# A transformer block's handover from the feed-forward up projection to the down projection: order of the vector work, request of the first activation pieces, and order of the first matmuls

## The reference, cut to what matters

```python
h = rmsnorm(x, ln_pre_ffn[layer])
u = causal_dwconv(h @ w_ffn_up[layer], conv_w[layer], conv_b[layer])
u_val, u_gate = jnp.split(u, 2, axis=-1)
f = jax.nn.gelu(u_gate, approximate=True) * u_val
x = x + rmsnorm(f @ w_ffn_down[layer], ln_post_ffn[layer])
```

## Time and profile before

| | us |
|---|---|
| median of 3 runs | 2316.39 |
| lowest and highest | 2311.63, 2318.4 |
| the profiled execution, its own time | 2311.12 |
| its span in the trace | 2309.3 |

### The profile page before, as it was taken

One profiled execution on the slowest core, in us unless ns is written; L12 is line 12 of the kernel. 1 busy time (PEld: TensorE's weight loads), 2 busy tenths in 40 slices (PEclk: granted clock), 3 DMA queues, 4 the chain that ended last, 5 costly groups with the idle time before them and its releaser, 6 DMA issues. The chain is left out here.

```text
span 2309.3 us, 26874 instructions
## 1 busy us (share of the span) xinstructions
PE 2267.7 (98%) x10222; PEld 1835.4 (79%) x10222; DVE 1192.5 (52%) x1229; ACT 607.1 (26%) x953; POOL 1613.9 (70%) x964
## 2 busy tenths in 40 slices
PE   8999999999999999999999999999999999999998
PEld 7888888888888888766666888878778888878887
DVE  7322222620488887333334444333867777785473
ACT  4323333211222221111112211114444444331211
POOL 5777776442666554866655368871999999989894
PEclk9999999999999999999999999999999999999999
DMA  4233333344233333544446656642222222245443
GB/s 176 100 110 110 110 110 110 116 175 149 89 103 105 110 114 125 174 144 142 147 143 194 199 201 224 232 169 101 82 74 82 83 83 82 92 146 209 140 147 150
DMA packets 175860, 308.95 MB, mean 134 GB/s; under 512 B 12352, under 2 KB 90432, under 8 KB 175744
## 3 DMA queue, kind: packets, MB, share of 16 engines
q1 hardware_dynamic: 175312, 306.27, 39.9%
q10 hardware_dynamic: 432, 1.11, 0.1%
HBM read 217.16 MB, written 90.18 MB: 133 GB/s over the span
## 5 line engine op out<-in xcount | busy, mean ns | idle before, releaser
L404 PE MATMUL psum<-act_hi,w_hi 128*128 128x512 f32 x1352 | 548.6, 406 | 2.7 <-POOL w_lo L2773 1.2
L406 PE MATMUL psum<-act_hi,w_lo 128*128 128x512 f32 x1352 | 528.7, 391 | 0.0
L405 PE MATMUL psum<-act_lo,w_hi 128*128 128x512 f32 x1352 | 527.2, 390 | 0.0
L438 POOL TENSOR_TENSOR w_hi<-w_raw,zero_col 128x1024 fp32r<-128x1024 f32 x101 | 207.1, 2050 | 246.1 <-PE psum L406 228.4
L404 PEld LDWEIGHTS psum<-act_hi,w_hi 128*128 128x128 f32 x1352 | 254.4, 188 | 60.6 <-issue 8.7
L405 PEld LDWEIGHTS psum<-act_lo,w_hi 128*128 128x128 f32 x1352 | 254.5, 188 | 57.2 <-issue 7.2
L406 PEld LDWEIGHTS psum<-act_hi,w_lo 128*128 128x128 f32 x1352 | 253.8, 188 | 54.6
L441 POOL TENSOR_TENSOR w_lo<-w_raw,w_hi 128x1024 fp32r<-128x1024 f32 x101 | 274.4, 2717 | 7.9
L1310 POOL TENSOR_TENSOR k_lev<-e_t,g_x 128x896 f32<-128x896 f32 x32 | 95.5, 2984 | 127.9 <-ACT e_t L1257 92.6
L404 PE MATMUL psum<-w_hi,act_hi 128*128 128x512 f32 x416 | 162.3, 390 | 1.7 <-POOL w_lo L441 1.4
L406 PE MATMUL psum<-w_hi,act_lo 128*128 128x512 f32 x416 | 161.9, 389 | 0.0
(11 more groups left out here) (279 smaller groups left out, 4670.4 us busy)
## 6 DMA issues: line engine op xcount, KB each, us to landing
w_raw<-in_w_stream SPq DMA_DIRECT2D x225, 512.0 KB, 4.2
proj_scratch<-stage SPq DMA_DIRECT2D x32, 512.0 KB, 5.2
proj_scratch<-side_out SPq DMA_DIRECT2D x64, 256.0 KB, 3.4
r_x<-proj_scratch SPq DMA_DIRECT2D x64, 256.0 KB, 3.2
value_scratch<-stage SPq DMA_DIRECT2D x24, 512.0 KB, 3.1
d_raw<-ffn_scratch SPq DMA_DIRECT2D x44, 256.0 KB, 3.7
ffn_scratch<-u_lin_v SPq DMA_DIRECT2D x20, 512.0 KB, 5.7
r_v<-value_scratch SPq DMA_DIRECT2D x32, 256.0 KB, 3.2
```

Source lines behind the costliest of these rows:

```text
L404: nc.tensor.matmul(o, s_hi, m_hi, start=start, stop=False)
L405: nc.tensor.matmul(o, s_hi, m_lo, start=False, stop=False)
L406: return nc.tensor.matmul(o, s_lo, m_hi, start=False, stop=stop)
L438: nc.gpsimd.tensor_tensor(w_hi[:, j, :], w_raw[:, j, :], zero_col[:, :].to_broadcast((P, D)), ALU.add).then_inc(sem["hi_split"], 1)
```

## The change

Four edits. VectorE: pair 21's sums `s16`, `s167`, `c21`, `add_5` go ahead of the first low part and of `f(19)`; `f(19)` comes after `c12`. SyncE: the wait ahead of pieces 0 to 3 asks for pair 21's product 4 low part, two GpSimd parts before the last. SyncE: `f_store(19)` goes from before slab 4's load to after piece 4's request. TensorE: pieces 0 and 1 are multiplied by row blocks, first (3, 1) of piece 0, (3, 1) of piece 1, then (0, 2) of piece 0 and (0, 2) of piece 1; `mm_half` is raised by 2 at the end of each of the last two.

```diff
         def down_pe(pe):
+            def rows_of(tok, q, slot, j, start, stop):
+                s_hi = d_hib[:, slot, tok * P:(tok + 1) * P]
+                s_lo = d_lob[:, slot, tok * P:(tok + 1) * P]
+                for cc in range(2):
+                    last = product3(psum[:, 2 * tok + cc, :], s_hi, s_lo, w_hi[:, j, cc * HALF:(cc + 1) * HALF],
+                                    w_lo[:, j, cc * HALF:(cc + 1) * HALF], start, stop)
+                return last
+
+            def first_pieces():
+                for toks in ((3, 1), (0, 2)):
+                    for q in range(2):
+                        if toks[0] == 3:
+                            pe.wait_ge(sem["slab_ready"], SL_DOWN + q + 1)
+                            pe.wait_ge(sem["d_lo"], q + 1)
+                        for tok in toks:
+                            if q == 0:
+                                for b in (2 * tok, 2 * tok + 1):
+                                    wait_evicted(pe, *UP_PRODS[N_PROD - 8 + (b + 12 - N_PROD) % 8])
+                            last = rows_of(tok, q, q, (q + SL_DOWN) % RING, q == 0, False)
+                        if toks[0] == 0:
+                            last.then_inc(sem["mm_half"], 2)
+
+            first_pieces()
...
-                repeat(pe, hf * FT, FT - hf * RING, body)
+                if hf == 0:
+                    for q in (2, 3):
+                        body(q, q, 0, q, False)
+                    repeat(pe, RING, FT - RING, body)
+                else:
+                    repeat(pe, FT, FT - RING, body)
...
-            sp.wait_ge(sem["u_lo"], AFTER_ROWS["u_lo"] + N_PROD)
+            sp.wait_ge(sem["u_lo"], AFTER_ROWS["u_lo"] + prod_index(FT - 1, 4) + 1)
             for k in range(RING):
                 sp.wait_ge(*f_stored(k))
                 piece(sp, k, 0, k)
-            f_store(sp, FT - 3)
             for k in range(RING):
                 n = SL_DOWN + RING + k
                 sp.wait_ge(sem["slab_ready"], n - RING + 1)
@@
                 sp.wait_ge(sem["d_lo"], k + 1)
                 sp.wait_ge(*f_stored(RING + k))
                 piece(sp, RING + k, 0, k)
+                if k == 0:
+                    f_store(sp, FT - 3)
...
             taps(p - 2, 1)
             taps(p - 2, 0)
-            f(p - 2)
-            split_lo(dve, 0, 0, True)
-            split_lo(dve, 1, 1, True)
             s16(p)
             s167(p)
             c21(p)
             add_5(p)
+            split_lo(dve, 0, 0, True)
+            up_c11(dve, p)
+            split_lo(dve, 1, 1, True)
+            c12(p)
+            f(p - 2)
             split_lo(dve, 2, 2, True)
-            up_c11(dve, p)
-            c12(p)
             split_lo(dve, 3, 3, True)
```

More of the change, by code:

```diff
@@ L2463, in body @@
                     j = (slot + SL_DOWN) % RING
-                    pe.wait_ge(sem["slab_ready"], k + (SL_DOWN + hf * FT + 1))
+                    pe.wait_ge(sem["slab_ready"], q + SL_DOWN + 1)
                     pe.wait_ge(sem["d_lo"], q + 1)
-                    start = isinstance(k, int) and k == 0
-                    stop = hf == 0 and isinstance(k, int) and k == FT - 1
+                    start = hf == 1 and isinstance(k, int) and k == 0
+                    stop = hf == 0 and isinstance(k, int) and q == FT - 1
                     for tok in range(4):
-                        if start and hf:
+                        if start:
                             pe.wait_ge(sem["d_evac"], tok + 1)
[L2471 to L2479, removed]
+                        last = rows_of(tok, q, slot, j, start, stop)
                         if tok % 2:
                             last.then_inc(sem["mm_half"], 1)
-                repeat(pe, hf * FT, FT - hf * RING, body)
+                if hf == 0:
[4 more added lines that the diff above has]
+                    repeat(pe, FT, FT - RING, body)
             for tok in range(4):
```

## The result

Over 13 runs each the changed kernel took 2319.57 us in the median (2317.34 to 2321.02), the kernel before 2313.75 (2311.08 to 2318.4). The ratio is 1.0022 with a 95% interval of 1.0014 to 1.0030: 3 to 7 us slower, about 5. The prediction was 2323.3 with a range of 2313 to 2328; on the later and lower median of before, its 6.9 us would have given 2320.7. By the prediction's bound of 0.3% the result is "the same". The interval does not contain 1, so a small slowdown is clear of the noise all the same.

A forecast was written before the change was run, and what follows sets the result against it. TensorE, busy 98%, was taken as the bound. The 7.75 us handover prize would be lost to an 11.6 us wait at piece 4 plus 2.75 of slow clock: 6.9 us later, 2316.39 + 6.9 = 2323.3, range 2313 to 2328.

The forecast's parts named there:

- bound of 0.3%: Whole kernel: the smallest difference its measurement can tell from no change, 6.95 us.
- cost of the slow clock: TensorE after the wait at piece 4: the clock falls again and costs 2.75 us, with 0 and 5.5 as ends.
- The relaxed wait is worth nothing: SyncE's queue ahead of pieces 0 to 3: the new wait brings no earlier request, still about 2040.8.
- The stall goes: TensorE ahead of piece 0: the 5.0 us wait on `add_5` and its 2.75 us of slow clock disappear.
- The pause goes: GpSimd ahead of slab 4: its idle stretch from 2061.11 to 2066.27 disappears, so VectorE's taps lose their free time.
- a turn: VectorE beside GpSimd: each instruction waits for a whole one of the other; taps take 2.3 to 3.3 us, not 1.27.
- near tie: VectorE's first tap of pair 20 against GpSimd's slab 4: whichever is first, the end is the same within 0.7 us.
- The sum: Start of piece 5: an 11.6 us wait at piece 4 and the slow clock make it 6.9 us later, 2094.65 against 2087.72.
- The row blocks: TensorE, pieces 0 and 1: 36 matmuls can start when the last product ends, at 2053.0; piece 0 finishes at 2061.2.
- Faster: Rival, VectorE's taps after 2061.9: they keep unhindered speed, the full 7.75 us are kept, 2308.6; chance 0.08.
- Nothing moves: Rival, TensorE at piece 0: starts late after all, up to 2057.8, and GpSimd's pause returns; 2315 to 2318; chance 0.11.
- Dearer: Rival, pieces 5 and 6: taps miss more turns or these pieces stall too, 3 to 6 us more, 2326 to 2329; chance 0.08.

The follow-up runs named there:

- sp_only: Only SyncE's two edits (relaxed wait, moved store of f(19)) put into the kernel before; 2313.2 us, ratio 0.9995 to the kernel before.
- hold_slab4: The changed kernel with one more wait, so GpSimd splits slab 4 only after f(20); 2311.87 us, ratio 0.9990 to the kernel before.
- dve_only: Only VectorE's new order put into the kernel before, with its TensorE and SyncE queues; 2319.05 us, ratio 1.0021 to the kernel before.
- order4_on_before: The kernel before with only the low and high parts of pieces 4 to 7 put earlier; 2313.11 us, ratio 0.9995 to the kernel before.

## Why the prediction was right

Set against the trace after, less its offset of 1.23 us:

| step | predicted | measured |
|---|---|---|
| pieces 0 to 3 asked | 2040.8 | 2040.74 |
| TensorE's first down matmul | 2053.0 | 2053.14 |
| low part of piece 0 done | 2051.1 | 2051.07 |
| `f(19)` done | 2056.8 | 2056.72 |
| GpSimd starts slab 4 | 2061.6 | 2061.73 |
| low part of piece 3 done | 2061.9 | 2061.82 |
| low part of piece 4 done | 2086.2 | 2085.90 |
| TensorE's wait at piece 4 | 11.6 | 10.87 |
| cost of the slow clock | 2.75 | 2.81 |
| start of piece 5 | 2094.65 | 2094.30 |

The slow clock's cost in the last but one row is piece 4's 8.25 us less 5.44.

**The relaxed wait is worth nothing**: right, by the rows and by sp_only. **The stall goes**: right. **The pause goes and the taps cost a turn each**: right, and hold_slab4 shows it by giving the pause back. The first tap was issued 0.02 us behind slab 4's high part, the near tie that the prediction named; in dve_only the tap was first and piece 4 still started within 0.13 us (2086.18 against 2086.05, each less its offset), so the order there does not matter, as it said. **The sum**: 6.9 us against 6.6 in the pair of traces. Of the difference, 0.3 is piece 4's low part, 0.1 the step from it to TensorE's matmul (0.15 where the prediction took 0.25), less 0.06 for the clock. That the wait is 0.8 shorter than predicted comes half from this and half from the four pieces before it, which ended at 2075.18 and not at 2074.8.

**The row blocks**: they were not needed. The prediction has TensorE start with the row blocks whose banks are free first; in dve_only it starts as soon (0.37 us of idle time) in the order of before, since VectorE has emptied each bank by the time it is needed.

The runs say somewhat less, 3.2 to 6.9 us by the interval, with 5.8 between the medians. The predicted time was off by 3.7 us, and 2.6 of these are its base: the median of three runs, 2316.39, where 13 runs gave 2313.75. Part of its being inside the range is thus the width of the range, which also took in no change at all; the mechanism and the shift are what the traces bear out.

What makes the runs of one kernel differ is in part the clock. Of the 35 runs of before beside sp_only, the 24 with a mean granted clock of 0.996 average 2313.4 us and the 10 with 0.995 average 2315.7. And the same stall does not always cost the same: behind the 4.9 to 5.0 us ahead of piece 0 the slow clock cost 2.75 us in the trace of before, 2.69 in sp_only and 1.73 in order4_on_before, where piece 0 took 7.17 us. How much of the difference between 6.6 and what the runs say comes from this stays open.

**The rivals.** Faster needed taps at 1.27 behind a running GpSimd instruction. That happened in no trace: a tap took 1.27 only with GpSimd idle or where the tap came first, as in dve_only, and then GpSimd paid. Nothing moves needed a late start: TensorE started at once. Dearer needed pieces 5 and 6 to stall too: GpSimd was idle for 9.19 us behind slab 7, VectorE ran alone, and they came in time.

## What to carry to other kernels

When a stall ahead of the bounding engine is removed, follow the other queues for as long as they were catching up under it: here the reserve of piece 5, 0.7 us, said that 7.75 us could not be kept. It did not say that the kernel would get slower. That came from the pause of 5.16 us which the stall had given VectorE, and which went with it. Two engines that take turns on a shared resource are each slowed by the other's early work. Holding back the one whose results are needed later and moving the urgent small instructions ahead of the long ones gave 7.3 us in the traces, 8 by the ratio, where the removal of the stall alone had cost 6.6 and 5.

## What the runs showed of the hardware

The price of the slow clock did not grow with the wait: 2.75 us behind 5.0 us of idle time, 2.81 behind 10.87, 2.39 behind 11.00 in dve_only. It differed behind nearly equal waits. Before, the clock fell within the stall (a mean of 0.64 from 2056 to 2058, with the restart at 2057.77) and cost 2.75. In order4_on_before, TensorE stood idle for 4.93 us and the clock fell only about the restart at 2059.65, for 1.73:

```profile
2056.00:2058.00 2.00, 0.00 (x0) 1.00 0.93 329
2058.00:2060.00 2.00, 0.35 (x1) 0.91 0.53 128
2060.00:2062.00 2.00, 2.00 (x6) 0.50 0.62 239
```

Waits of 1.50, 1.61 and 1.84 us left the clock at 1.00. Waits of 3.20 and 3.22 did not; in hold_slab4 the clock fell only after TensorE was back at work (it restarted at 2086.40), so a row with a fast first matmul does not show that the clock was kept:

```profile
2086.00:2088.00 2.00, 1.60 (x7) 0.93 0.28 80
2088.00:2090.00 2.00, 2.00 (x6) 0.50 0.90 326
2090.00:2092.00 2.00, 2.00 (x8) 0.71 0.61 250
```

Between the last product and the first matmul of the down projection the kernel has `eng.drain()`, which no row of before could show by itself. In all nine traces in which TensorE starts there without a wait, it is idle for 0.37 us, and the profile names no engine that it waits for; that the drain is the reason is not shown separately.
